# First expert products: two products of 512 and 256 columns against three products of 256

## The reference, cut to what matters

```python
def token_block(args):
    xb, ib, gb = args                       # tokens, picked experts, gates
    u = jnp.take(expert_u, ib, axis=0)
    act = jax.nn.gelu(jnp.einsum('td,tkd->tk', xb, u).astype(jnp.float32), approximate=False)
    vv = jnp.take(expert_v, ib, axis=0)
    return jnp.einsum('tk,tkd->td', (gb * act).astype(h.dtype), vv)
```

## Time and profile before

| | before |
|---|---|
| median of 3 runs | 1297.62 us (1295.9 to 1298.31) |
| span of the profiled execution, first to last instruction | 1296.0 us |
| PE busy | 1284.0 us (99%), 7048 matmuls |
| PEld busy | 1089.6 us (84%) |
| DVE busy | 986.4 us (76%) |
| ACT busy | 650.7 us (50%) |
| granted TensorE clock | full in all 40 slices |

### The profile page before, as it was taken

One profiled execution on the slowest core, in us unless ns is written; L12 is line 12 of the kernel. 1 busy time (PEld: TensorE's weight loads), 2 busy tenths in 40 slices (PEclk: granted clock), 3 DMA queues, 4 the chain that ended last, 5 costly groups with the idle time before them and its releaser, 6 DMA issues.

```text
span 1296.0 us, 17206 instructions
## 1 busy us (share of the span) xinstructions
PE 1284.0 (99%) x7048; PEld 1089.6 (84%) x7048; DVE 986.4 (76%) x1265; ACT 650.7 (50%) x624; POOL 105.9 (8%) x142
## 2 busy tenths in 40 slices
PE   9999999999999999999999999999999999999998
PEld 6888878888789888988888888888888888888887
DVE  7557779889876875699989899997576666666663
ACT  6555563344455455464555565565454444444441
POOL 0101200000020000000000011011120000000000
PEclk9999999999999999999999999999999999999999
DMA  9515379996453134556777779998998787887860
GB/s 378 202 60 195 128 301 418 381 377 221 162 212 131 65 140 185 165 192 228 237 237 226 238 240 300 295 301 291 339 358 329 288 290 290 291 292 290 291 228 33
DMA packets 113726, 318.30 MB, mean 246 GB/s; under 512 B 7280, under 2 KB 74096, under 8 KB 92016
## 3 DMA queue, kind: packets, MB, share of 16 engines
q1 hardware_dynamic: 94944, 247.98, 53.8%
q0 software_dynamic: 18416, 68.17, 14.7%
q10 hardware_dynamic: 288, 1.05, 0.2%
HBM read 282.56 MB, written 34.61 MB: 245 GB/s over the span
## 4 chain that ended last, share of the span: by engine, by line
PE 89%; DVE 6%; ACT 2%; DMA 1%; issue 1%; POOL 0%; SPq 0%; DVEq 0%; ACTq 0%
PE psum L519 87%; PE psum L522 2%; DVE slab_lo L1687 2%; DMA hidden_store<-arena 1%; ACT arena L1379 1%; DMA slab_raw<-in_w_in 0%; ACT slab_hi L1246 0%; DVE arena L1982 0%; ACT arena L1287 0%; DVE arena L2243 0%; ACT arena L1249 0%; ACT arena L1269 0%; DVE arena L1946 0%; DVE residual L2432 0%; POOL statistics L466 0%
## 5 line engine op out<-in xcount | busy, mean ns | idle before, releaser
L1687 DVE TENSOR_TENSOR slab_lo<-slab_raw,slab_hi 128x2048 fp32r<-128x2048 f32 x206 | 469.4, 2287 | 176.4 <-ACT slab_hi L1246 176.4
L1246 ACT ACTIVATE slab_hi<-slab_raw 128x2048 fp32r<-128x2048 f32 x206 | 392.7, 1912 | 232.2 <-PE psum L519 226.7
L519 PE MATMUL psum<-slab_hi,x_parts 128*128 128x512 f32 x1520 | 480.8, 392 | 2.5 <-ACT x_parts L1293 0.9
L519 PE MATMUL psum<-x_parts,slab_hi 128*128 128x512 f32 (+1 forms) x1344 | 420.3, 371 | 1.1 <-DVE arena L2229 1.1
L519 PEld LDWEIGHTS psum<-slab_hi,x_parts 128*128 128x128 f32 x1520 | 285.4, 188 | 65.2 <-issue 5.6
L519 PE MATMUL psum<-x_parts,slab_lo 128*128 128x256 f32 x1184 | 330.9, 279 | 0.0
L519 PE MATMUL psum<-slab_lo,x_parts 128*128 128x512 f32 x760 | 295.9, 389 | 0.0
L519 PEld LDWEIGHTS psum<-x_parts,slab_hi 128*128 128x128 f32 x1344 | 241.8, 188 | 46.3 <-DVE arena L2229 1.7
L519 PEld LDWEIGHTS psum<-x_parts,slab_lo 128*128 128x128 f32 x1184 | 223.6, 189 | 0.0
L519 PEld LDWEIGHTS psum<-slab_lo,x_parts 128*128 128x128 f32 x760 | 142.8, 188 | 28.8 <-issue 0.2
L519 PE MATMUL psum<-slab_hi,weighted_hi 128*128 128x512 f32 x296 | 116.0, 392 | 0.1
(11 more groups left out here) (276 smaller groups left out, 1049.5 us busy)
## 6 DMA issues: line engine op xcount, KB each, us to landing
slab_raw<-in_ex_u SPq DMA_DIRECT2D x128, 512.0 KB, 5.5
slab_raw<-in_ex_v SPq DMA_DIRECT2D x64, 1024.0 KB, 6.4
arena<-in_w_ada SPq DMA_DIRECT2D x24, 1024.0 KB, 7.1
slab_raw<-in_w_gu SPq DMA_DIRECT2D x22, 1024.0 KB, 7.1
slab_raw<-in_w_in SPq DMA_DIRECT2D x21, 1024.0 KB, 8.7
hidden_store<-arena POOLq DMA_DIRECT2D x32, 512.0 KB, 5.6
arena<-hidden_store POOLq DMA_DIRECT2D x32, 512.0 KB, 5.3
arena<-gates_store POOLq DMA_DIRECT2D x32, 512.0 KB, 6.6
```

The lines of the kernel that those rows point to most:

```text
L519: return PE.matmul(out, lhsT, rhs, start=start, stop=stop)
L1246: ACTE.activation(slab_hi[:, slot, :], raw[:, slot, :], ACT.Copy).then_inc(hi_made[slot], 1)
L1687: DVE.tensor_tensor(slab_lo[:, slot, :], raw[:, slot, :], slab_hi[:, slot, :].bitcast(f32), ALU.subtract).then_inc(lo_made[slot], 1)
```

## The change

The three products of a (m, k) become three matmuls of 256 columns into the same 256 columns of PSUM, so PSUM itself adds them. m = 0 takes columns 0 to 255 of one bank and m = 1 columns 256 to 511 of it. A half now does 32 matmuls with the high weights and then 16 with the low weights, and waits for the low part of the slab only between the two. ACT applies gelu from PSUM straight to `hidden_out`, half by half. The copy of the rest and DVE's sum are gone, with the space `hidden_low` that they used.

```diff
             def expert_half(bank, n):
-                take(n)
-                bh, bl = parts(n % NSLOT, KT, S)
+                slot = n % NSLOT
+                PE.wait_ge(hi_made[slot], n // NSLOT + 1)
+                bh, bl = parts(slot, KT, S)
                 for m in range(2):
-                    col = slice(m * P, m * P + P)
+                    col, o = slice(m * P, m * P + P), ps[:, bank, m * S:m * S + S]
                     for k in range(KT):
-                        mm(ps[:, bank + m, :], bh[:, k, col], xx[:, :, k, :], k == 0, False)
-                        ins = mm(ps[:, bank + m, 0:S], bl[:, k, col], xh[:, k, :], False, k == KT - 1)
+                        mm(o, bh[:, k, col], xh[:, k, :], m == 0 and k == 0, False)
+                        mm(o, bh[:, k, col], xl[:, k, :], False, False)
+                PE.wait_ge(lo_made[slot], n // NSLOT + 1)
+                for m in range(2):
+                    col, o = slice(m * P, m * P + P), ps[:, bank, m * S:m * S + S]
+                    for k in range(KT):
+                        ins = mm(o, bl[:, k, col], xh[:, k, :], False, m == 1 and k == KT - 1)
                 used(ins, n)
...
                 else:
-                    PE.wait_ge(*after("hidden_summed", s - 1))
+                    PE.wait_ge(*after("hidden_made", s - 1))
                 expert_half(2 * (s % 2), S_EU + s)
...
             def store_hidden(c):
-                POOL.wait_ge(*after("hidden_made", c + 1))
+                POOL.wait_ge(*after("hidden_made", 2 * c + 2))
...
-            def hidden_gelu(c):
-                ACTE.wait_ge(*after("hidden_summed", 2 * c + 2))
-                ACTE.activation(hidden_out[c % 2], hidden_out[c % 2], ACT.Gelu).then_inc(sem("hidden_made"), 1)
+            def hidden_gelu(c, half):
+                if half == 0 and c >= 2:
+                    ACTE.wait_ge(*after(f"hidden_stored{c % 2}", 16 * (c // 2)))
+                ACTE.activation(hidden_out[c % 2][:, 2 * half:2 * half + 2, :].rearrange("p a t -> p (a t)"),
+                                ps[:, 2 * half, :], ACT.Gelu).then_inc(sem("hidden_made"), 1)
...
                 slab_done(ACTE, S_EU + s)
-                if s >= 2:
-                    ACTE.wait_ge(*after("hidden_summed", s - 1))
-                ACTE.activation(hidden_low(s), ps[:, 2 * half:2 * half + 2, S:2 * S], ACT.Copy).then_inc(
-                    sem("hidden_low_copied"), 1)
+                hidden_gelu(c, half)
...
-            def expert_sum(s):
-
-                c, q = divmod(s, 2)
-                DVE.wait_ge(*after("hidden_low_copied", s + 1))
-                if q == 0 and c >= 2:
-                    DVE.wait_ge(*after(f"hidden_stored{c % 2}", 16 * (c // 2)))
-                DVE.tensor_tensor(hidden_out[c % 2][:, 2 * q:2 * q + 2, :], ps[:, 2 * q:2 * q + 2, 0:S], hidden_low(s),
-                                  ALU.add).then_inc(sem("hidden_summed"), 1)
-
             def prepare(n):
-                s = n - S_EU - NSLOT
-                if 0 <= s < 2 * EX_N:
-                    expert_sum(s)
                 lo(n)
```

More of the change, by code:

```diff
@@ L146 @@
     "mixed_x_hi": (("mem_early_hi", 1), ("mem_late_hi_for_k", 1), ("pool_x_hi", 1), ("fox_x_hi", 1),
-                   ("mem_late_hi_for_v", 1), ("mem_x_hi", 2), ("mix_x_hi", 4), ("hidden_low_copied", 2 * EX_N)),
+                   ("mem_late_hi_for_v", 1), ("mem_x_hi", 2), ("mix_x_hi", 4)),
     "mixed_x_lo": (("mem_early_lo", 1), ("mem_late_lo_for_k", 1), ("pool_x_lo", 1), ("fox_x_lo", 1),
-                   ("mem_late_lo_for_v", 1), ("mem_x_lo", 2), ("mix_x_lo", 4), ("hidden_summed", 2 * EX_N)),
+                   ("mem_late_lo_for_v", 1), ("mem_x_lo", 2), ("mix_x_lo", 4)),
     "late_constants": (("first_slab_half_loaded", 16), ("output_gains_loaded", 16)),
@@ L332, in program @@
         LAST_HIT = 2 * EX_N - 7
-        def hidden_low(s):
-            flat = wf[:] if s < GATE_FROM else zs[:] if s >= LAST_HIT else carve(10240, 1024)
-            return flat[:, (s % 2) * 512:(s % 2) * 512 + 512].rearrange("p (a t) -> p a t", a=2)
         hidden_store = nc.dram_tensor("hidden_store", (EX_N, P, EX_A * S), f32).ap()
@@ L501, in gpsimd_program @@
                         POOL.wait_ge(*after(f"gates_stored{k}", 16 * (S // GATE_T // 2)))
-                    POOL.wait_ge(*after("hidden_summed", LAST_HIT))
                 for n in range(3):
@@ L1656, in scalar_program @@
                         ACTE.activation(dst, ps[:, bank, 0:S], ACT.Copy).then_inc(sem("choice_copied"), 1)
-                if half:
-                    if c:
-                        hidden_gelu(c - 1)
                 hi(S_EU + s + 4)
@@ L1672, in scalar_program @@
                     weighted_hi(c + 1)
-                if c == 0:
-                    hidden_gelu(EX_N - 1)
                 for n in range(S_EV + 2 * c + 4, min(S_EV + 2 * c + 6, S_END)):
@@ L2377, in gate_step @@
                     DVE.wait_ge(*after("hits_used", 2 * (i - 2) + 2))
-                if i == 1:
-                    DVE.wait_ge(*after("hidden_summed", GATE_FROM))
                 shape = [P, 8 // NEXT, NKEYS, NEXT]
```

## The result

The changed kernel takes 1306.41 us (median of 4 runs, 1305.98 to 1306.93) against 1296.80 for the kernel before (4 runs, 1295.90 to 1298.31). The ratio is 1.007, 95% interval 1.0057 to 1.0082. It is 9.6 us (0.7%) slower, where 9.4 were forecast, and the time lies inside the range and 0.6 us under the 1307.0 forecast.

A forecast was written before the change was run, and what follows sets the result against it. The prediction took PE's stream of matmuls to bound the stage. +10.8 us for the triples and -1.4 for the stalls made +9.4, so 1297.6 + 9.4 = 1307.0 us; 1303 to 1310 by the first term's ends, stated range 1302 to 1313.

The forecast's parts named there:

- The triple for the pair: PE's first expert products: 1024 groups go from 0.3495 to 0.360 us each, +10.8 us, with ends +6.8 and +13.8.
- The formula that the prediction set beside it: Skill's matmul gap, columns / 2.4 + 2.5 ns, leaving out weight loads; would make the extra matmuls cost +2.6 us.
- the fast pairs: Stretch of PE's stage before with pairs at 0.3465 us; all pairs at that would make the triple's term +13.8 us.
- The sum: Whole kernel: +10.8 for the triples and -1.4 for the stalls make +9.4 us.
- the stalls: PE's two waits for DVE's sum in the stage, 0.78 and 0.63 us, both go: -1.4 us.
- The pair costs 0.3495 in two instructions, and the triple 0.360 in three.: PE, per (m, k): same 768 columns before and after, but every group gets 0.0105 us longer.
- DVE and ACT: DVE loses 64 sums, 43.5 us; ACT saves 33 us, or 5 at the upper end; off the path except the stalls.
- The low part's later wait: PE's wait for slab_lo moves from a half's start to behind 32 matmuls; gives nothing.
- Rival 1: Changed stage: 256-column triples go slower under transfer load, 0.367 us, +3.6 to +7.2 more, 1311 to 1314; chance 0.09.
- Rival 2: PE's stage: only columns count, triples cost 0.3465 us like fast pairs, -4.5 with the stalls, 1293.1; chance 0.05.
- rival 3: PE's stage: only a small cost per instruction, a third of 0.0105 per group, +2.2, 1299.8; chance 0.07.
- Rival 4: POOL's queue: a hidden store behind a gates block lands late, gelu then PE wait; +16 at 28 us, 1323; chance 0.03.

The follow-up runs named there:

- e1: Kernel before with only its 512-column matmul cut into two of 256; copy, sum and gelu kept: 1306.92 us, ratio 1.0081.
- e4: The changed kernel run again, unedited, beside other runs on the same chip: 1305.92 us, ratio 1.0071 to the kernel before.
- e5: Changed kernel with each 256-column matmul cut into two of 128 columns: 1621.61 us (one run).
- e10: Changed kernel with matmuls of 128 columns and stationary operands of 64 columns, half of the first expert products left out: 1305.48 us (one run).
- e2: Changed kernel with the old pairs, grouped by kind, no sums, high-by-low product left out of the result: 1294.16 us, ratio 0.9981 to the kernel before.
- e7: Kernel before with stationary operands of 64 columns, half of the first expert products left out: 1287.97 us (one run).
- e6: Changed kernel with stationary operands of 64 columns where it has 128, half of the first expert products left out: 1292.86 us (one run).
- e9: Kernel before with pairs grouped by kind and DVE's sum and low part one piece earlier in the top-16 selection: 1295.38 us, ratio 0.9986.
- e3: Changed kernel with the three products of each step together and both waits at the half's start: 1306.25 us, ratio 1.0074 to the kernel before.
- e8: Kernel before with only the order changed, 16 matmuls of 512 columns then 16 of 256 per half: 1295.99 us, ratio 0.9993.

## Why the prediction was right, point by point

**The triple for the pair: +10.8.** Right, and to its size. The three products stand 0.120 apart in the stage as they did in the query products. The stage's 400.02 us, less 28.8 for gate steps, 0.4 for selections and 28 restarts of 0.08, leaves 368.6 us, which is 1024 x 0.360. Before it was 357.9, so the term is +10.7. e1 shows the cause: this edit alone makes 1306.92. It came out because the price was read from rows of the same instruction with the same operands and not worked out from columns. The formula that the prediction set beside it would have given +2.6 for the term. Against the fast pairs alone the triple's term is +13.8; it came out 3 lower because a part of the pairs of before ran at 0.3534. The prediction took that mean as it stood and did not say why pairs have two spacings, and that is still open.

**The sum: +9.4, measured +9.6.** That these agree to 0.2 us is in part luck. In the stage, where everything forecast takes place, the change made +9.05: the triples 10.7, less 1.4 for the stalls and 0.2 for their two restarts, which the sum had left standing. The measured 9.6 holds scatter of the size of the difference: e4 has 1305.92 against 1296.73, which is 9.2.

**"The pair costs 0.3495 in two instructions, and the triple 0.360 in three."** As a sum this held. As a reason it is half of it. e5 against e10 rules out a fixed price per instruction: with loads of 128 columns, matmuls of 128 columns stand 0.112 apart, with loads of 64 columns 0.060. At 512 columns the load's size does not show: 0.228 in e2 with full loads, 0.23 in e7 with half. In between, at 256 columns, full-size loads have 0.120, and small ones settle at 0.113 in the 8-column stream and in e6 after its first interruption. So the likely reason is that loads of 128 columns leave little room there (0.112 in 0.120), and that the third instruction matters by the load it brings. This is argued and not shown, because of the first part of e6. Why it is 0.120 and not 0.113 or 0.112 stays open.

**The stalls: -1.4.** The stalls went, as forecast, but the reason given was not needed. The prediction had them go because the gelu does not stand behind the top-16 selection. In e1 the sums stand where they stood, and all but 0.14 us of the stalls is gone too, likely because halves that are 0.1 to 0.2 us longer give DVE the time it lacked. In e9 the sums are all there and no stall is left, by DVE's order. So nearly all of the -1.4 comes with the split alone. The removal of the sums adds at most the 0.25 us between the stages of e1 and e4.

**DVE and ACT.** DVE had 43.5 us less to do and ACT 33, by forecast. In the stage DVE went from 351.7 to 316.8 and ACT from 219.4 to 191.6 (in a stretch that is 9.4 us longer and has 63 gelus). The sums' durations added up, 64 x 0.68, are the 43 us that were forecast. Consecutive spans on DVE overlap in the profile, and busy time counts the overlap once, so it falls by less, 35. A gelu of 512 columns from PSUM takes 0.598 us, the lower of the two bounds, in this row of the groups on ACT:

```profile
L1644 ACT ACTIVATE arena<-psum 128x512 f32<-128x512 f32 x63 | 37.7, 598 | 204.0 <-PE psum L513 204.0
```

**The low part's later wait.** Right: nothing (e3 against e4, 0.3 us).

**The rivals.** Rival 1 (triples slower under load) is out: they stand at 0.120 with transfers at 0.78. Rival 2 (only columns count) and rival 3 (a small price) are out by the same rows. Rival 4 had its mechanism right and its consequence not, by a narrow margin. POOL issues the stores of chunks 18 and 21 right behind a block of gates:

```profile
783.34 1.71 POOL L472 DMA_DIRECT2D gates_store<-arena  x1 [16.55 <-ACT arena L1629]
785.04 0.55 POOL L467 DMA_DIRECT2D hidden_store<-arena  x1
```

The store of chunk 18 took 11.8 us to land and was there 3.1 us before the gelu of half 40, which needs it. The store of chunk 21 was the longest of all, 13.8 us, and landed at 841.67. The gelu of half 46, which needs it, came only 0.5 us later, and the 3.42 us that ACT had waited went to PE:

```profile
827.92 0.55 POOL L467 DMA_DIRECT2D hidden_store<-arena  x1
...
842.16 0.60 ACT L1644 ACTIVATE arena<-psum 128x512 f32<-128x512 f32 x1 [3.42 <-PE psum L513]
```

In e4 the margin there was 0.1 us. So no gelu waited for a store, but an earlier gelu would have.

## What to carry to other kernels

Where TensorE is full, count its matmuls and their weight loads as well as its columns: a float32 matmul of 256 columns with its own 128-column load took 0.120 us where half of one of 512 took 0.114. Putting two operands side by side so that one load serves 512 columns was worth 10 us here, and the copies and sums of 512 columns that it makes necessary cost 1 us at most, because they stand on engines that are not the bound. Price a rearranged matmul from rows of the same shape in the same trace.

## What was not expected of the hardware

- The same instructions can have two spacings, and a long stream can hold one of them. Pairs of 512 and 256 columns run at 0.3465 or 0.3534, and in e6 the matmuls ran at 0.120 for 1152 of them and at 0.1133 after two transposes. What sets the spacing is not known.
- Grouped by kind (e8), the pairs have one spacing, 0.348, and the kernel's 11 runs lie within 1.0 us where the 15 of the kernel before spread over 3.5. That the two spacings make the spread may be, but it is not shown.
- Using the same stationary operand in the next matmul saves nothing: it is loaded again (8072 loads for 8072 matmuls), and both of the "x2" matmuls take 0.120.
- A full load row says little: it was full at 0.120 and at 0.1133 in e6, and at 0.060 in e10.
